# The last layer norm with tokens on partitions, its result stored in eight half blocks from two queues

## What is computed

```
u = causal_dwconv(x @ w_up, f_conv_w, f_conv_b)
u_gate, u_val = split(u, 2)
x = layer_norm(ALPHA * x + (silu(u_gate) * u_val) @ w_down, ln2_g, ln2_b)
return x        # (1, 512, 1024)
```

## Time and profile before

| | |
|---|---|
| time before, median of 3 runs | 2582.67 us (2580.94 to 2585.09) |
| profiled execution | 2586.92 us |
| its span (first to last instruction) | 2585.1 us |
| TensorE busy | 2513.1 us, 97% |
| VectorE, ScalarE, GpSimd busy | 1369.7, 667.3, 1563.8 us |
| granted TensorE clock, mean | 0.988 of 2.4 GHz |

### The profile page before, as it was taken

One profiled execution on the slowest core, in us unless ns is written; L12 is line 12 of the kernel. 1 busy time (PEld: TensorE's weight loads), 2 busy tenths in 40 slices (PEclk: granted clock), 3 DMA queues, 4 the chain that ended last, 5 costly groups with the idle time before them and its releaser, 6 DMA issues.

```text
span 2585.1 us, 30721 instructions
## 1 busy us (share of the span) xinstructions
PE 2513.1 (97%) x11112; PEld 1990.6 (77%) x11112; DVE 1369.7 (53%) x1916; ACT 667.3 (26%) x1101; POOL 1563.8 (60%) x1061
## 2 busy tenths in 40 slices
PE   7999999999999999999999999999999999999998
PEld 6875688888877776688867886867888777888876
DVE  5975683221379999968214426344356244534534
ACT  3006621100254434421022114133114121300102
POOL 2640257766779898667643765624764467666653
PEclk8999999999999999999999999999999999999999
DMA  9620132333222322122321231311332222233321
GB/s 298 222 94 1 52 123 86 98 98 98 98 82 82 97 73 74 53 98 96 105 76 33 98 98 46 103 49 53 98 94 66 65 82 93 70 98 98 89 96 47
DMA packets 224141, 231.46 MB, mean 90 GB/s; under 512 B 12219, under 2 KB 213788, under 8 KB 223900
## 3 DMA queue, kind: packets, MB, share of 16 engines
q1 hardware_dynamic: 221104, 229.33, 28.0%
q10 hardware_dynamic: 2924, 0.66, 0.1%
HBM read 227.87 MB, written 2.10 MB: 89 GB/s over the span
## 4 chain that ended last, share of the span: by engine, by line
PE 85%; DVE 8%; DVEq 2%; ACT 2%; POOLq 1%; issue 1%; POOL 1%; DMA 1%; ACTq 0%; SPq 0%
PE PS L1540 64%; PE PS L1487 7%; DVE PS L3076 3%; PE PS L1348 3%; PE PS L2136 1%; DVEq L3078 1%; PE PS L1007 1%; PE PS L2338 1%; PE PS L2355 1%; PE PS L2127 1%; DVE PS L3120 1%; PE PS L2723 1%; DMA spare<-in_ada_w 1%; POOLq L1457 1%; PE PS L1777 0%
## 5 line engine op out<-in xcount | busy, mean ns | idle before, releaser
L1461 POOL TENSOR_TENSOR Wl<-raw,Wh 128x512 fp32r<-128x512 f32 (+1 forms) x764 | 1035.2, 1386 | 28.1 <-issue 0.5
L1455 POOL TENSOR_SCALAR Wh<-raw 128x2048 fp32r<-128x2048 f32 (+1 forms) x195 | 367.6, 1886 | 808.9 <-issue 370.9
L1540 PE MATMUL PS<-Hh,Wh 128*128 128x512 f32 x1936 | 765.9, 396 | 29.3 <-POOL Wl L1461 20.9
L1540 PE MATMUL PS<-Hl,Wh 128*128 128x512 f32 x1936 | 758.7, 392 | 0.0
L1540 PE MATMUL PS<-Hh,Wl 128*128 128x512 f32 x1936 | 758.5, 392 | 0.0
L1540 PEld LDWEIGHTS PS<-Hh,Wh 128*128 128x128 f32 x1936 | 366.5, 189 | 116.0 <-POOL Wl L1461 20.3
L1540 PEld LDWEIGHTS PS<-Hl,Wh 128*128 128x128 f32 x1936 | 366.8, 189 | 78.0 <-issue 1.9
L1540 PEld LDWEIGHTS PS<-Hh,Wl 128*128 128x128 f32 x1936 | 366.3, 189 | 77.5
L1540 PE MATMUL PS<-Bh,Wh 128*128 128x512 f32 x640 | 249.4, 390 | 2.1 <-POOL Wl L1461 2.1
L1540 PE MATMUL PS<-Bh,Wl 128*128 128x512 f32 x640 | 249.0, 389 | 0.0
L1540 PE MATMUL PS<-Bl,Wh 128*128 128x512 f32 x640 | 249.0, 389 | 0.0
(11 more groups left out here) (497 smaller groups left out, 3091.7 us busy)
## 6 DMA issues: line engine op xcount, KB each, us to landing
raw<-in_w_in SPq DMA_DIRECT2D x44, 1024.0 KB, 5.4
raw<-in_w_ff SPq DMA_DIRECT2D x32, 1024.0 KB, 5.3
raw<-in_conv_w_in SPq DMA_DIRECT2D x24, 1024.0 KB, 5.2
raw<-in_ret_w_in SPq DMA_DIRECT2D x24, 1024.0 KB, 5.1
spare<-in_ada_w SPq DMA_DIRECT2D x20, 1024.0 KB, 8.9
raw<-in_w_up SPq DMA_DIRECT2D x20, 1024.0 KB, 5.3
raw<-in_w_out SPq DMA_DIRECT2D x8, 1024.0 KB, 4.9
raw<-in_conv_w_out SPq DMA_DIRECT2D x8, 1024.0 KB, 5.0
```

Source lines behind the costliest of these rows:

```text
L1455: pool.tensor_scalar(st.Wh[0:rows, slot, k, 0:cols], st.raw_slot(slot)[0:rows, k, 0:cols], 1.0, 1.0, ALU.mult, ALU.mult)
L1461: ins = pool.tensor_tensor(st.Wl[0:rows, slot, k, 0:cols], st.raw_slot(slot)[0:rows, k, 0:cols], st.Wh[0:rows, slot, k, 0:cols].bitcast(F3 ...
L1540: mm = pe.matmul(out, lhs, rhs, start=(k == parts[0][0] and n == 0), stop=(k == parts[-1][0] and n == 2))
```

## The change

`CentredNorm` (for `ln2` only) and `store_part` are replaced by one class, `LastNorm`.

- The last `w_down` segment becomes four phases written out in one round. In its fourth tile the column blocks run one after the other (`bank_by_bank`), with a signal `first_bank` after block 0; the other tiles keep their order.
- Within TensorE's third and fourth tile, chunks 0 to 3, 4 and 5, and 6 of X are transposed to PSUM (`raw`), and after the last tile chunk 7. VectorE takes each token's counts, means and variances from there (`bn_stats`, joined by `bn_aggr`).
- ScalarE multiplies each chunk by the gain (features are still on partitions) into `scaled`; TensorE transposes these 8 chunks as 32 blocks into eight half banks of tokens by 512 features (`turn_scaled`).
- Minus the mean, and (variance + eps) times the reciprocal deviation, are made for each token as two columns, each in high and low part (`columns`), turned into rows by 4 transposes, and multiplied by 6 rows of gain and bias (`factors`); this product is accumulated onto the transposed chunks (`add_means`, 8 products of 512 columns). The reciprocal deviation is then a scale per partition.
- VectorE scales the left halves (features 0 to 511) of the four token blocks, and SyncE stores each; ScalarE scales the right halves and issues the store of each itself. So there are eight DMAs of 256 KB.
- The rows of gain and bias are loaded and rounded in a part of its own, `prepare`, for SyncE and VectorE. It stands behind the first three entries of the feed-forward list, that is between the `w_down` segment of group 0 and the `w_up` segment of group 1. The scratch that it writes is in `st.A`.

```diff
-        downs.append(tiles(wd, F, 4, 0, row0=g * D, rows=rows, ready=made,
-                           dve=add_to_x(st, x_scale=ALPHA if g == 0 else 1.0)))
+        add = add_to_x(st, x_scale=ALPHA if g == 0 else 1.0)
+        if g == n_groups - 1:
+            downs.append(Seg(wd, F, 1, [Phase(p * TW, dve=add) for p in range(4)], row0=g * D, rows=rows, ready=made))
+        else:
+            downs.append(tiles(wd, F, 4, 0, row0=g * D, rows=rows, ready=made, dve=add))
...
-            ln2 = CentredNorm(nc, st, "l2", ffn[-1], 1e-5, pcols("ln2_g_3", 8), pcols("ln2_b_3", 8))
+            ln2 = LastNorm(nc, st, t, out, ffn[-1], 1e-5, pcols("ln2_g_3", 8), t["ln2_g_3"], t["ln2_b_3"], ln1.ready(7))
             return [
                 z0, z, y_squares, gb[0], y_norm, gb[1],
-                p_b, w_out, ln1.part, *ffn, ln2.part,
-                store_part(nc, st, out, lambda c: (ln2.hi_in, c + 1))]
+                p_b, w_out, ln1.part, *ffn[:3], ln2.prepare, *ffn[3:], ln2.part]
...
+    def load_rows(self, sp):
+        sp.wait_ge(self.cleared, 1)
+        sp.dma_start(self.rows[0:3, :], self.gain_row.to_broadcast([3, D])).then_inc(self.rows_in, 16)
+        sp.dma_start(self.rows[3:6, :], self.bias_row.to_broadcast([3, D])).then_inc(self.rows_in, 16)
+
+    def make_rows(self, dve):
+        dve.wait_ge(*self.rows_free)
+        dve.memset(self.rows, 0.0)
+        dve.memset(self.columns.bitcast(F32), 0.0)
+        dve.tensor_tensor(self.low_row, self.st.ident[:, 1:2], self.st.ident[:, 4:5], ALU.add)
+        dve.drain().then_inc(self.cleared, 1)
+        dve.tensor_scalar(self.sign, self.low_row, -2.0, 1.0, ALU.mult, ALU.add)
+        dve.wait_ge(self.rows_in, 32)
+        dve.tensor_copy(self.rounded, self.rows)
...
+    def within_bank(self, pe, p, b, k):
+        if (p, b, k) == (2, 0, 3):
+            self.raw(pe, (0, 1, 2, 3))
+        if (p, b, k) == (3, 0, 3):
+            self.raw(pe, (4, 5))
+        if (p, b, k) == (3, 1, 3):
+            self.raw(pe, (6,))
...
+    def counts_before_last(self, dve, i, p):
+        self.count(dve, 0)
+        dve.wait_ge(self.first_bank, 1)
+        self.add(dve, self.st.PS[:, 2 * self.own_slot(), :], 6).then_inc(self.seventh_in, 1)
+        self.count(dve, 1)
+        self.count(dve, 2)
...
+    def tensor(self, pe):
...
+        turn_scaled(0, 0)
+        self.raw(pe, (7,))
+        for b in range(1, NB):
+            turn_scaled(b, 0)
+        pe.wait_ge(self.counted, 3 * NB)
+        for b in range(2):
+            turn_scaled(b, 1)
+        pe.wait_ge(self.columns_in, 1)
...
+        mm.then_inc(self.columns_turned, 1)
+        turn_scaled(2, 1)
+        pe.wait_ge(self.rows_made, 1)
+        pe.wait_ge(self.columns_copied, 1)
+        add_means(0, 0)
+        add_means(0, 1)
+        turn_scaled(3, 1)
...
+    def scalar(self, act):
...
+        for b in range(NB):
+            act.wait_ge(self.filled, 2 * b + 2)
+            act.activation(self.Y[:, b, 4 * P:], st.PS[:, self.bank(b, 1), :], ACT.Copy,
+                           scale=self.rstd[:, b:b + 1]).then_inc(self.right_out, 1)
+            act.wait_ge(self.right_out, b + 1)
+            act.dma_start(to[:, b, 4 * P:], self.Y[:, b, 4 * P:]).then_inc(self.stored, 16)
...
+    def vector(self, dve):
+        st = self.st
+        self.count(dve, 3)
...
+        for b in range(NB):
+            dve.wait_ge(self.filled, 2 * b + 1)
+            dve.tensor_scalar(self.Y[:, b, 0:4 * P], st.PS[:, self.bank(b, 0), :], self.rstd[:, b:b + 1], None,
+                              ALU.mult).then_inc(self.left_out, 1)
```

More of the change, by code:

```diff
@@ L1179, in __init__ @@
         self.k_order, self.pieces = None, pieces
+        self.bank_by_bank, self.first_bank, self.within_bank = (), None, None
         self.widths = None
@@ L1513, in seg @@
                     if g.mode != "tokens" else [(b, TW) for b in range(NB)]
-                if g.mode == "tokens":
+                bank_by_bank = p in g.bank_by_bank
+                if g.mode == "tokens" or bank_by_bank:
                     order = [(k, rows, b, m) for b, m in blocks for k, rows in parts]
@@ L1524, in seg @@
                         g.within(pe, i, p, k)
+                    if g.within_bank:
+                        g.within_bank(pe, p, b, k)
                     if early and b == 0:
@@ L1541, in seg @@
                                        stop=(k == parts[-1][0] and n == 2))
+                    if bank_by_bank and b == 0 and k == parts[-1][0]:
+                        mm.then_inc(g.first_bank, 1)
                 mm.then_inc(multiplied, 1)
@@ L2898, in group_norm_parts @@
     return squares, part
[L2901 to L2912, removed]
-        for c in range(KC):
[L2914 to L2922, removed]
-        for b in range(NB):
[L2924 to L2945, removed]
@@ new lines, with __init__, x_in, own_slot @@
+class LastNorm:
+    def __init__(self, nc, st, t, out, seg, eps, gain, gain_row, bias_row, rows_free):
+        self.st, self.t, self.out, self.seg, self.eps, self.gain = st, t, out, seg, eps, gain
+        self.gain_row, self.bias_row, self.rows_free = gain_row, bias_row, rows_free
+        self.ctx = ExitStack()
+        (self.cleared, self.rows_in, self.rows_made, self.first_bank, self.seventh_in, self.turned, self.counted,
+         self.gained, self.var_in, self.rstd_in, self.columns_in, self.columns_turned, self.columns_copied,
+         self.filled, self.left_out, self.right_out, self.stored) = sems(
+            nc, self.ctx, "l2", "cleared rows_in rows_made first_bank seventh_in turned counted gained var rstd "
+                                "columns columns_turned columns_copied filled left_out right_out stored")
+        A = st.A
+        self.rows = A[:, 10:12, :].rearrange("p c n -> p (c n)")
+        self.rounded = st.early[:, 12:14, :].rearrange("p c n -> p (c n)")
+        self.factors = st.early[:, 14:16, :].rearrange("p c n -> p (c n)")
+        self.columns = st.late[:, 12, :].rearrange("p (b n) -> p b n", b=NB)
+        self.spread = st.late[:, 13, :].rearrange("p (b n) -> p b n", b=NB)
+        small = lambda a, n: A[:, 30, a:a + n]
+        self.counts = small(0, 96).rearrange("p (b g n) -> p b g n", b=NB, g=4)
+        self.moments = small(96, 8).rearrange("p (b n) -> p b n", n=2)
+        self.pair = small(104, 8).rearrange("p (b n) -> p b n", n=2)
+        self.log, self.rstd = small(112, 4), small(116, 4)
+        self.low_row, self.sign = small(120, 1), small(121, 1)
+        self.scaled = st.spare[:, 8:16, :]
+        self.Y = st.spare[:, 0:8, :].rearrange("p (b c) n -> p b (c n)", b=NB)
+        seg.bank_by_bank, seg.first_bank, seg.within_bank = (3,), self.first_bank, self.within_bank
+        seg.phases[2].more = self.counts_before_last
+        seg.phases[3].dve = self.last_chunk
+        self.prepare, self.part = Part(ExitStack()), Part(self.ctx)
+        self.prepare.sync(self.load_rows)
+        self.prepare.vector(self.make_rows)
+        self.part.tensor(self.tensor)
+        self.part.scalar(self.scalar)
+        self.part.vector(self.vector)
+        self.part.sync(self.sync)
+    def x_in(self, c):
+        return (self.seventh_in, 1) if c == 6 else (self.seg.posted, self.seg.posted_at(0, c // 2))
+    def own_slot(self):
+        return (self.seg.base + 3) % 2
+    def bank(self, b, half):
+        own, other = self.own_slot(), 1 - self.own_slot()
+        return 4 + b if half == 0 else (2 * other, 2 * other + 1, 2 * own, 2 * own + 1)[b]
+    def load_rows(self, sp):
[11 more added lines that the diff above has]
+        dve.tensor_copy(self.rounded, self.rows)
+        dve.drain()
+        dve.tensor_scalar(self.rows, self.rows, self.low_row, None, ALU.mult)
+        dve.drain()
+        dve.scalar_tensor_tensor(self.factors, self.rounded.bitcast(F32), self.sign, self.rows, ALU.mult,
+                                 ALU.add).then_inc(self.rows_made, 1)
+    def turn(self, pe, out, c, b):
+        return pe.transpose(out, self.st.X[:, c, b * P:(b + 1) * P], self.st.ident)
+    def raw_bank(self, c, b):
+        PS = self.st.PS
+        at = lambda k, n: PS[:, k, n * P:(n + 1) * P]
+        if c < 4:
+            return at(4 + b, c)
+        if c < 6:
+            return at(self.bank(b // 2, 1), 2 * (b % 2) + c - 4)
+        return at(self.bank(2 + c - 6, 1), b)
+    def raw(self, pe, chunks_of):
+        for c in chunks_of:
+            pe.wait_ge(*self.x_in(c))
+            for b in range(NB):
+                mm = self.turn(pe, self.raw_bank(c, b), c, b)
+        mm.then_inc(self.turned, 1)
+    def within_bank(self, pe, p, b, k):
[5 more added lines that the diff above has]
+            self.raw(pe, (6,))
+    def count(self, dve, n):
+        dve.wait_ge(self.turned, n + 1)
+        PS = self.st.PS
+        for b in range(NB):
+            view = (PS[:, 4 + b, :], PS[:, self.bank(b // 2, 1), (b % 2) * 2 * P:(b % 2) * 2 * P + 2 * P],
```

(80 more changed lines are left out.)

## The result

The changed kernel takes 2592.79 us (median of 9 runs, 2589.23 to 2598.12) against 2582.95 us (9 runs): the ratio is 1.004, with a 95% interval of 1.003 to 1.0051. So it is 0.4% slower, 9.8 us by the medians. The forecast was 2591.5 us, 8.8 us above the median of the first three runs.

What follows compares the result with a forecast made beforehand. TensorE's weight products were taken to bound the kernel up to 2557.46 us, then a 27.64 us hand-to-hand tail. Stall 16.9 + clock 2.2 - 10.3 (tail less transposes) = +8.8 us on 2582.67: 2591.5 us, range 2585 to 2598.

Steps and rivals of the forecast that it cites:

- The stall: At the second `w_up` group, SyncE's wait on `cleared` delays the weight tile and TensorE: 16.9 us, bounds 15.7 to 18.
- The lower clock: Behind the gap TensorE restarts at half clock, eleven products 0.43 us apart: 2.2 us lost, bounds nothing to 4.7.
- The last down projection: 28 transposes between TensorE's products add 2.9 us, a dropped column sum saves 0.86: last product ends 2.1 us later.
- The waits for chunks 4 to 6: In the last down projection, TensorE's waits for VectorE before transposing these chunks: costed at nothing.
- The prediction's warning: In the last down projection, `bn_stats` at twice its rows' price makes TensorE wait about 1.5 us for chunk 6.
- The tail: From last product to end of span: 15.25 us instead of 27.64, 12.4 less.
- The store's two queues: In the final store, issuing from ScalarE too adds no bandwidth; if queues added up, the end would be 1.2 us sooner.
- No stall: Rival: at the second `w_up` group SyncE finds `cleared` already given, only the tail counts, -10.3 us, 2572.4; chance 0.09.
- The stall with a larger gain: Rival: stall holds, but the tail gains 13 or the clock costs nothing: +3.9 us, 2586.6, within 0.2%; chance 0.11.
- A small gain of the tail: Rival: slow `bn_stats`, ScalarE alternation or idle engines between stores leave a 3 us gain: +16.1 us, 2598.8; chance 0.05.

Runs made afterwards that it cites:

- experiment 1: The changed kernel with VectorE's two memsets and small addition that give `cleared` moved to the start of the last feed-forward; 2575.14 us, 0.9962 of the kernel before.
- experiment 2: The kernel before with only the early step `prepare` added, its rows used by nobody; 2604.51 us, ratio 1.0079.
- experiment 6: The kernel of experiment 1 with SyncE's row loads also waiting for the third double add of the first down projection; 2582.66 us, ratio 0.9995.
- experiment 7: The kernel of experiment 1 with SyncE's row loads also waiting for the second double add of the first down projection; 2572.33 us, ratio 0.9959.
- experiment 3: The changed kernel with 72 unused filler matmuls of 128 columns on TensorE in the gap heading the second group; 2591.66 us, ratio 1.0036.
- experiment 4: The kernel of experiment 1 with all eight half-block stores issued by SyncE, ScalarE only scaling; 2573.05 us, ratio 0.9961.

## Why the prediction was right

- *The stall, 16.9.* Right in place and mechanism (experiments 1, 2, 6, 7). In the changed kernel the first product comes 17.56 us late (2342.72 against 2325.47 - 0.31, the distance of the earlier trace rows), 0.66 more than forecast; with the filler it is 17.9. The pieces: VectorE's signal 3.3 us after the start of the last add (forecast 3.1), 1.1 to the tile's issue (0.9), 5.7 to the split (5.3, which was the landing alone, without GpSimd's start), 7.1 for the split (7.2 with the hand-over).
- *The lower clock, 2.2.* Right in kind, somewhat less: 1.85 behind the gap, of which experiment 3 ties 1.7 to the idleness; eight slow products and not eleven.
- *The last down projection, 2.1.* It was 2.64. The 28 transposes cost 3.06 against 2.9 and the sum that went is 0.86, which is 2.2; the rest lies in the fourth tile, whose order bank after bank I had put at nothing. This tile takes 10.50 - 1.31 of transposes = 9.19 us, and took 9.58 - 0.86 = 8.72 before. With its start the tile now has four changes between row parts of 128 and of 64 rows instead of two (each starts its product about 0.1 us late), and one more break for transposes. That this is the whole of the 0.47 is argued and not shown. The waits for chunks 4 to 6 were hidden as forecast; TensorE waited for none. The prediction's warning that `bn_stats` at twice its price would make TensorE wait some 1.5 us does not come out of its own rows. Counted from the start of the tile: adds to 1.4, four at 1.28 to 6.5, the add of chunk 6 to 7.2, against a request at 7.0 (27 products and 8 transposes); that is 0.2. Nothing in the sum hung on it.
- *The tail, 15.25.* It was 14.56. The sum up to the first store was 0.6 too long: 0.3 of it in `bn_stats` (0.22 for each 128 columns against 0.29), 0.3 in the five small VectorE operations (0.84 against 1.1); the store was as computed (7.35), 7.2 us.
- *The store's two queues.* The rule of the Trainium skill held (experiment 4).
- *Rivals.* No stall: it would have been 10.4 us faster, and experiment 1 makes such a kernel, at 2575.14 us. The stall with a larger gain: the tail fell by 13.1 and not 12.4, but the other terms took it back. A small gain of the tail: no.

The total is nearer than its terms. By the profile the stall and the clock together cost 0.3 us more than forecast and the down projection 0.5 more, and the tail gained 0.7 more; these misses cancel, and leave 8.97 against 8.8. That the sum is so close is luck; where the stall lies, what releases it and what the tail gains are not.

The kernel of experiment 1 beats both the kernel before and the changed one; one queue or two is the same for it.

## What to carry to other kernels

A part that loads a constant is not free because it is small: where it stands in the load queue's program decides, and a wait in it on a compute engine pulls the queue back to where that engine is. Before such a step is put in, read how far the queue runs ahead (here 25 us) and what the next load needs from its issue to its use (here 13 us: 5.7 to the split and 7.1 for it). What counts is how much later the load goes out than it would have, and not how long the queue stands. The delay is free up to the difference of the two, here 12 us, and after that it costs its full excess: counted from the last add against experiment 1, the tile went out 6 us later in experiment 7 (no gap), 17 in experiment 6 (a gap of 5.5, with the slower split in it) and 30 in the changed kernel (17.6). The lower clock behind the gap comes on top. The store here, which filled the DMA engines, gained from an earlier first byte, and not from a second queue.

## What was not expected of the hardware

- A wait of 2.06 us on TensorE, which every one of these kernels has at the first `w_down` tile of the second group, has two outcomes. In the kernel before and the changed one the granted clock stays at 1.00 behind it, and in eight of the nine profiled executions the products behind it are 0.23 apart. In that of experiment 2 the clock is 0.50, seven products go 0.43 apart, and the last product ends 1.5 us later than the stall explains, with the same products and the same wait:

```profile
2496.00:2498.00 2.00, 0.10 (x1) 0.14 (x1) 1.02 (x2) 0.87 (x2) 2.00 (x3) 0.97 0.01 4
2498.00:2500.00 2.00, 2.00 (x5) 1.61 (x6) 1.85 (x4) 0.00 (x0) 1.85 (x2) 0.50 0.54 135
```

  That can be one of the sources of a spread of some microseconds between executions; with one trace for each kernel, how often it comes is not shown.
- VectorE's passes from SBUF to SBUF and GpSimd's split slow each other. The three passes over 1024 columns take 0.69, 0.75 and 1.28 us in the changed kernel's gap, and 0.85, 1.60 and 2.13 us in experiment 1, where GpSimd splits beside them. It is not TensorE's work that slows them: in experiment 3 it runs the filler beside them and GpSimd stands, and they take 0.69, 0.75 and 1.28 again. The other way round, in experiment 6 the two passes of the split, 1.92 and 5.03 us otherwise, took 5.83 us in one tile's second and 2.87 in the next tile's first.
